# Prompt index products of a hybrid decoder layer: full rows, and index queries held for one tile

## The chip, the cores and the metric

The kernel runs on one core of one Trainium2 chip. It is written by hand for the five engines, each with its own instruction stream: PE (TensorE), DVE (VectorE), ACT (ScalarE), POOL (GpSimd) and SP (SyncE, which here only issues transfers). Semaphores order them. The metric is the device time of one execution in microseconds; three timed runs of the kernel before gave 3959.62, 3966.36 and 3967.23 us, a median of 3966.36.

## The reference

One decoder layer over 2048 prompt tokens and 64 sample tokens: a combined projection, then attention over keys that an indexer picks, beside a state-space branch, an output projection and a squared-relu MLP. The change touches the indexer for the prompt:

```python
def indexer_topk(qi, wi, ki, q_pos, topk):
    s = jnp.einsum('bqhd,bld->bqhl', qi, ki) * (IDX_DIM ** -0.5)      # 4 heads of 64
    score = jnp.einsum('bqhl,bqh->bql', jax.nn.relu(s), wi) * (N_IDX_HEADS ** -0.5)
    score = jnp.where(admissible[None], score, -jnp.inf)
    _, idx = lax.top_k(score, topk)                                    # topk = 256
```

For every block of 128 queries this is done against all keys up to the block's end. All of it is in float32. The four heads share one set of index keys of 64 dimensions. Positive factors on the score change nothing in the choice, and the kernel leaves them out.

## The kernel before

The prompt is cut into 16 tiles of 128 tokens. Tiles 0 and 1 need no choice. The others are chosen in four groups, `SELECT = ((2, 3), (4, 5, 6, 7), (8, ..., 11), (12, ..., 15))`. A tile passes through three steps of a search pipeline: its scores are made, then ACT counts the upper 19 bits of a threshold while the next tile's scores are made, then DVE counts the lower 13 bits and builds the mask while a third tile's scores are made. The third of these steps is shared by no more than three tiles, so `score` has three buffers.

Scores of a tile `t` are made in pieces, `(h, u)`: head `h` of 4, and a stretch `u` of 1024 keys, that is up to two banks of 512. A piece is one `matmul` per bank on PE (`index`, line 1567), one relu per bank on ACT (line 1889, from PSUM into `relu`, two buffers), and one multiply-and-add with the head's weight on DVE (`combine`, line 2159). PSUM banks of the products are a ring of four, `sring`, made of the banks `sc` and `tr` that attention uses at other times. A 32-bit product is recorded as two LDWEIGHTS and two MATMUL records, whose buffer names are `kiT` (keys) and `qi` (queries).

`kiT` holds the 64 dimensions of the index keys twice, in partitions 0 to 63 and 64 to 127. The queries are in DRAM as `qi_d[t]`, 128 partitions x 2 x 128: partitions 0 to 63 hold heads 0 and 2, partitions 64 to 127 heads 1 and 3. A product for head `h` takes the half `h % 2` of both, 64 rows:

```python
rows = slice(HD * (h % 2), HD * (h % 2) + HD)
pe.matmul(sring[i % SRING][:, 0:w], qi[rows, n % 2, h // 2, :], R["kiT"][rows, 512 * b:512 * b + w], ...)
```

The order of all work is one list, `plan`, that every engine walks through in the same order, each doing its own part of a unit. It merges the main stream, the units of the projection and the MLP (`W`, `N`, `M`, `U` for an up chunk of 24 products, `D` for down products, `E`), with the side stream, units of search `("S", s, p, k)` and of attention `("A", s, j)`, by rough costs. In `("S", s, p, k)`, `s` is the group, `p` the step of the pipeline and `k` the tick within it. While `p` is 0, a piece goes out at every tick; from `p` = 1 on, at every second tick of 20, since search rounds lie between. The last piece of a group's first tile and the first piece of its second are thus next to each other in the plan: for tiles 4 and 5 nothing lies between, nor for tiles 2 and 3 and tiles 8 and 9; for tiles 12 and 13 one `D` unit of twelve down products does. Tile 8's pieces have one up unit in their midst, and tile 9's first piece has one right behind it.

SP walks the same plan and issues transfers in order; where it has to wait, all that is behind it waits too. `load_index` (line 1345) is one of them, beside weights (`raw`, line 1279), features (`xs`), masks and queries of attention. At the start of a group it first waits until attention's last outputs of the group before are stored (line 1385), since both use the same memory. `qi` has two buffers with a semaphore each, so tile t+1's queries are asked for while tile t's predecessor is in work.

Of the kernel before, what the change touches and what calls it, by code (L numbers as in the profile page):

```python
# [6 lines left out]
ACT = mybir.ActivationFunctionType  # L7
# [7 lines left out]
P = 128  # L15
# [11 lines left out]
HD = 64  # L27
# [393 lines left out]
class Count:  # L421
# [9 lines left out]
    def wait(self):  # L431
        self.eng.wait_ge(self.sem, self.n)
# [350 lines left out]
def blend(nc, A, ident, par):  # L783
# [262 lines left out]
    with ExitStack() as ctx:  # L1046
# [32 lines left out]
        at[0] = side  # L1079
        qi = place_at("qi", [P, 2, 2, P])  # L1080
        relu = place_at("relu", [P, 2, 1024])
# [119 lines left out]
        x2_st, y_st = [sem(f"x2_st{i}_") for i in range(5)], [sem(f"y_st{i}_") for i in range(5)]  # L1201
        qi_ld, mask_st = [sem("qi_ld0_"), sem("qi_ld1_")], [sem("mask_st0_"), sem("mask_st1_")]
        s_full, s_free, comb_ok, causal_ok, trial_ok, count_ok, mask_ok, own = (
# [63 lines left out]
        with nc.Block() as block:  # L1267
            @block.sync
            def _(sp):
# [75 lines left out]
                def load_index(t):  # L1345
                    n = turn_s[t]
                    if n >= 2:
                        sp.wait_ge(s_full, n_index[t])
                    sp.dma_start(qi[:, n % 2], A["qi_d"][t]).then_inc(qi_ld[n % 2], 16)

                n_index, seen = {}, []
                for ts in SELECT:
                    for t in ts:
                        seen.append(t)
                        n_index[t] = index_bank[seen[-3], NIH - 1, banks(seen[-3]) - 1] + 1 if len(seen) > 2 else 0

# [23 lines left out]
                def select_part(s, p, k):  # L1380
                    ts = SELECT[s]
                    if p == 0 and k == 0:
                        if s:
                            for i in range(2):
                                sp.wait_ge(aT_st[i], 16 * 2 * s)
                        load_index(ts[0])
                        load_index(ts[1])
                    if 1 <= p and k == 0 and p + 1 < len(ts):
                        load_index(ts[p + 1])
                    if p >= 2 and k == LOWER + CHOICE - 1:  # L1390
                        t = ts[p - 2]
                        n = turn_s[t]
                        sp.wait_ge(mask_ok, n + 1)
                        sp.dma_start(m_d[t, :, 0:width(t)], tie[:, 0:width(t)]).then_inc(mask_st[n % 2], 16)
# [93 lines left out]
            def _(pe):  # L1488
# [78 lines left out]
                def index(s, p, k):  # L1567
                    ts = SELECT[s]
                    if p >= len(ts) or k % piece_step(p) or k // piece_step(p) >= len(pieces(ts[p])):
                        return  # L1570
                    t = ts[p]
                    h, u = pieces(t)[k // piece_step(p)]
                    n = turn_s[t]
                    pe.wait_ge(qi_ld[n % 2], 16 * (n // 2 + 1))
                    rows = slice(HD * (h % 2), HD * (h % 2) + HD)
                    for b in range(2 * u, min(2 * u + 2, banks(t))):
                        i = index_bank[t, h, b]
                        wait(pe, s_free, i - SRING + 1)
                        w = part_w(width(t), 512, b)
                        pe.matmul(sring[i % SRING][:, 0:w], qi[rows, n % 2, h // 2, :], R["kiT"][rows, 512 * b:512 * b + w],  # L1580
                                  start=True, stop=True).then_inc(s_full, 1)
# [180 lines left out]
            def _(act):  # L1762
# [114 lines left out]
                def select_part(s, p, k):  # L1877
# [3 lines left out]
                    if p < len(ts) and k % piece_step(p) == 0 and k // piece_step(p) < len(pieces(ts[p])):  # L1881
# [4 lines left out]
                        for b in range(2 * u, min(2 * u + 2, banks(t))):  # L1886
                            i, w = index_bank[t, h, b], part_w(width(t), 512, b)
                            act.wait_ge(s_full, i + 1)
                            act.activation(relu[:, r % 2, 512 * (b - 2 * u):512 * (b - 2 * u) + w], sring[i % SRING][:, 0:w],
                                           ACT.Relu).then_inc(s_free, 1)  # L1890

# [590 lines left out]
```

## Time and profile before

| | |
|---|---|
| median of three runs | 3966.36 us |
| profiled execution | 3963.13 us, its span 3961.5 us |
| PE busy | 3229.5 us, 82% |
| DVE / ACT / POOL busy | 2167.9 / 1850.8 / 1266.4 us |
| mean granted clock of PE | 0.891 of full |
| index products, in the two groups of records of 512 columns | 224 records, 131.8 us |
| loads of `qi` | 14, of 128 KB each |

The span is the time between the first and the last record; the execution's own time is a little longer. Busy shares are means over a kernel that has stages of different kinds: the input projection up to about 350 us, the state-space branch up to about 560, the sample tokens and the first search up to about 1040, then three rounds in which search and attention lie beside the MLP, and from about 3050 us on the last quarter of the MLP. Index products lie between 569 and 2782 us. The granted clock in the slices is a mean over 99 us each: 9 or less means that some of the slice was spent at the lower level.

### The profile page before, as it was taken

How to read it: one execution, taken by the hardware profiler on the slowest of the kernel's cores; microseconds unless marked ns; L12 is line 12 of the kernel's file. 1: busy time of each engine (PE TensorE's matmuls, PEld its weight loads, DVE VectorE, ACT ScalarE, POOL GpSimd, SP SyncE). 2: the span in 40 equal slices, each digit the busy share in tenths (PEclk: the TensorE clock that was granted, in tenths of full speed). 3: DMA queues.
4: the chain of work that ended last, by engine and by line, in shares of the span. 5: the costliest groups of instructions: out<-in, count | busy, mean ns of one | idle time of the engine just before them, and what ended most of it. 6: DMA issues, size and time to landing. Idle time of an engine off the chain costs nothing.

```text
span 3961.5 us, 47273 instructions
## 1 busy us (share of the span) xinstructions
PE 3229.5 (82%) x15388; PEld 2447.5 (62%) x15388; DVE 2167.9 (55%) x4196; ACT 1850.8 (47%) x3065; POOL 1266.4 (32%) x1134
## 2 busy tenths in 40 slices
PE   7996536258778899886888998777788999889997
PEld 6885422134555677654666776555566777668885
DVE  4434934942357864367886333677785333553334
ACT  3323325513456645565664446656654444433333
POOL 1334401122024541243254013422463110324544
PEclk9997768577889889988899999988898999989998
DMA  4444245344232221123222111242222110432222
GB/s 155 138 138 160 50 144 136 86 153 148 83 124 66 69 83 51 48 70 141 73 81 73 52 33 57 69 148 69 69 69 85 38 42 25 147 117 80 80 85 72
DMA packets 198864, 357.36 MB, mean 90 GB/s; under 512 B 55690, under 2 KB 113100, under 8 KB 197180
## 3 DMA queue, kind: packets, MB, share of 16 engines
q1 hardware_dynamic: 180092, 327.81, 25.9%
q0 software_dynamic: 9312, 18.14, 1.4%
q10 hardware_dynamic: 9216, 8.39, 0.7%
q8 instruction: 124, 2.03, 0.2%
q14 instruction: 120, 0.98, 0.1%
HBM read 294.44 MB, written 67.01 MB: 91 GB/s over the span
## 4 chain that ended last, share of the span: by engine, by line
PE 42%; DVE 20%; issue 11%; ACT 6%; POOL 3%; DMA 2%; SPq 1%; ACTq 1%; POOLq 0%; DVEq 0%
PE r L1564 9%; PE r L1532 8%; PE po L1613 7%; PE r L1505 3%; PE tr L1604 3%; DVE junk_v_b L2233 3%; PE sc L1592 3%; DVE trial_b L2185 3%; POOL acc_b L1999 2%; DVE dn_b L2080 2%; DVE up_b L2080 2%; PE sc L1591 2%; ACT junk_a_b L1874 1%; ACT dn_b L1769 1%; PE r L1676 1%
## 5 line engine op out<-in xcount | busy, mean ns | idle before, releaser
L1564 PE MATMUL r<-dn_b,h_b 128*128 128x512 f32 x2880 | 767.6, 424 | 174.9 <-ACT part_b L1825 84.7
L1564 PEld LDWEIGHTS r<-dn_b,h_b 128*128 128x128 f32 x2880 | 574.9, 205 | 353.9 <-ACT part_b L1825 103.3
L1999 POOL TENSOR_TENSOR acc_b<-acc_b,part_b 128x512 f32<-128x512 f32 x375 | 514.5, 1392 | 605.4 <-ACT part_b L1825 604.8
L1532 PE MATMUL r<-x_hi_b,up_b 128*128 128x512 f32 x2048 | 660.8, 396 | 6.8 <-DVE x_lo_b L2099 4.2
L1874 ACT ACTIVATE junk_a_b<-score_b,trial_b 128x384 int8<-128x384 f32 (+13 forms) x266 | 348.1, 1309 | 303.5 <-DVE trial_b L2185 291.8
L1532 PEld LDWEIGHTS r<-x_hi_b,up_b 128*128 128x128 f32 x2048 | 389.6, 190 | 105.5 <-issue 15.6
L1980 POOL TENSOR_TENSOR hr_b<-hr_b 128x512 f32<-128x512 f32 x128 | 146.6, 1145 | 852.9 <-ACT hr_b L1812 852.9
L1532 PE MATMUL r<-x_lo_b,up_b 128*128 128x512 f32 x1024 | 402.8, 393 | 0.0
L1825 ACT ACTIVATE part_b<-r 128x512 f32<-128x512 f32 x390 | 224.4, 594 | 239.6 <-PE r L1564 163.2
L1903 ACT ACTIVATE pT_b<-tr 128x512 f32<-128x512 f32 (+3 forms) x320 | 169.0, 528 | 331.9 <-PE tr L1604 330.2
L1613 PE MATMUL po<-V_sb,pT_b 128*128 128x64 f32 x2176 | 314.0, 285 | 1.7 <-DVE o_b L2250 1.4
L1613 PEld LDWEIGHTS po<-V_sb,pT_b 128*128 128x128 f32 x2176 | 272.1, 194 | 66.7 <-issue 53.8
L2080 DVE TENSOR_TENSOR dn_b<-raw_b,dn_b 128x1024 fp32r<-128x1024 f32 x120 | 171.9, 1433 | 237.3 <-ACT dn_b L1769 236.3
L2080 DVE TENSOR_TENSOR up_b<-raw_b,up_b 128x1024 fp32r<-128x1024 f32 x136 | 196.7, 1446 | 190.6 <-ACT up_b L1769 190.0
L2264 DVE CUSTOM_DVE_ANT_0 prob_b<-sc,mk_b,mx_b 128x512 f32<-128x512 f32 (+3 forms) x192 | 125.0, 651 | 306.2 <-PE sc L1592 306.1
L2233 DVE TENSOR_SCALAR_CACHE_REDUCE junk_v_b<-score_b,trial_b 128x384 bf16<-128x384 f32 (+13 forms) x182 | 268.0, 1472 | 1.3
L1988 POOL TENSOR_TENSOR h_b<-hr_b,h_b 128x512 fp32r<-128x512 f32 x128 | 219.6, 1716 | 132.1 <-ACT h_b L1841 132.1
L1532 PEld LDWEIGHTS r<-x_lo_b,up_b 128*128 128x128 f32 x1024 | 195.1, 190 | 39.1
L2264 DVE CUSTOM_DVE_ANT_0 prob_b<-sc,mk_b 128x512 f32<-128x512 f32 (+3 forms) x128 | 82.2, 642 | 242.4 <-PE sc L1592 218.4
L1909 ACT ACTIVATE prob_b<-prob_b,nmx_b 128x128 f32<-128x128 f32 (+15 forms) x128 | 153.9, 1202 | 110.4 <-DVE nmx_b L2270 108.8
L1604 PE MATMUL tr<-ident_sb,prob_b 128*128 128x128 f32 x1088 | 181.0, 283 | 12.5 <-ACT prob_b L1909 11.7
L375 PE MATMUL pp<-w_hi_sb,xT_hi_sb 128*128 128x512 f32 (+2 forms) x512 | 178.9, 349 | 5.9 <-ACT w_raw_sb L203 5.9
(385 smaller groups left out, 5749.7 us busy)
## 6 DMA issues: line engine op xcount, KB each, us to landing
raw_b<-w_up SPq DMA_DIRECT2D x128, 512.0 KB, 3.7
raw_b<-w_down SPq DMA_DIRECT2D x128, 512.0 KB, 3.6
raw_b<-w_out SPq DMA_DIRECT2D x64, 256.0 KB, 3.0
kv_b<-kv_pages SPq DMA_DIRECT2D x96, 128.0 KB, 3.8
kv_b<-kv_pages POOLq DMA_DIRECT2D x96, 128.0 KB, 3.7
x_tok_sb<-x_all SPq DMA_DIRECT2D x17, 512.0 KB, 4.6
xT_sb<-xT_all SPq DMA_DIRECT2D x17, 512.0 KB, 4.9
kic<-kidx_d SPq DMA_DIRECT2D x4, 2048.0 KB, 8.8
```

The source lines that it names most:

```text
L375: mm = pe.matmul(pp[j][:, 0:b - a], x[:, t % 2, k, :], w[:, k, a:b], start=n == 0, stop=n == 3 * KD - 1)
L1532: mm = pe.matmul(x[:], wt[:, c], y[:, k], start=k == n == 0, stop=(k, n) == (KD - 1, 2))
L1564: mm = pe.matmul(x[:], f[:, tok], w[:, col], start=c == n == 0, stop=(c, n) == (KQ - 1, 2))
L1604: mm = pe.transpose(x[:, (k - 4 * b) * P:(k - 4 * b + 1) * P], prob[:, n % 2, k * P:(k + 1) * P], ident[:])
L1613: mm = pe.matmul(po[:, h, :], pT[:, prob_no[t, h, b] % 3, k - 4 * b, :], R["V"][:, k, n:n + HD], start=k == 0, stop=k == t)
L1825: act.activation(dst, ring[bank_no[key] % RING][:], ACT.Copy).then_inc(free_act, 1)
L1874: act.activation(junk_a[:, 0:width(t)], score[:, n % 3, 0:width(t)], ACT.Sign, bias=trial[:, 0:1].bitcast(F32), accum_out=count[:, 0:1]).t ...
L1988: pool.tensor_tensor(z, s, a.bitcast(F32), ALU.subtract).then_inc(h_lo_ok, 1)
L1999: pool.tensor_tensor(dst, dst, part[:, add_no[key] % 2, :], ALU.add).then_inc(add_pool, 1)
L2080: dve.tensor_tensor(lo, raw_of(x), hi.bitcast(F32), ALU.subtract).then_inc(lo_ok, 1)
L2233: c.step(dve.tensor_scalar(junk_v[:, 0:width(t)], score[:, turn_s[t] % 3, 0:width(t)], trial[:, lower_trial(t)].bitcast(F32), 0.0, ALU.is_ ...
L2264: dve.tensor_tensor_reduce(out=prob[:, n % 2, 512 * b:512 * b + w], in0=sc[i % 2][:, 0:w], in1=mk[:, t % 2, 512 * b:512 * b + w], scale=1. ...
```

## The change

Three things are changed. First, each head's queries are placed in both halves of the partitions, so `qi` is `[P, NIH, P]` and holds one tile instead of two, in the same room. A product then takes all 128 rows: the keys stand twice in `kiT`, so the sum is twice the product, and the relu behind it has `scale=0.5`. Second, `load_index` issues four transfers of 64 partitions x 2 x 128 in place of one of 128 x 256: two halves of the partitions, for the even and the odd heads each. Third, as there is one buffer, a tile's load waits until the last product of the tile before it has ended, and it stands in the plan behind the last piece of that tile instead of one tile earlier; there is one semaphore, `qi_ld`, that counts 64 per tile.

```diff
-        qi = place_at("qi", [P, 2, 2, P])
+        qi = place_at("qi", [P, NIH, P])
...
-        qi_ld, mask_st = [sem("qi_ld0_"), sem("qi_ld1_")], [sem("mask_st0_"), sem("mask_st1_")]
+        qi_ld, mask_st = sem("qi_ld"), [sem("mask_st0_"), sem("mask_st1_")]
...
                 def load_index(t):
-                    n = turn_s[t]
-                    if n >= 2:
-                        sp.wait_ge(s_full, n_index[t])
-                    sp.dma_start(qi[:, n % 2], A["qi_d"][t]).then_inc(qi_ld[n % 2], 16)
+                    wait(sp, s_full, n_index[t])
+                    for z in range(2):
+                        for h in range(2):
+                            sp.dma_start(qi[HD * z:HD * z + HD, h::2], A["qi_d"][t, HD * h:HD * h + HD]).then_inc(qi_ld, 16)
...
-                        n_index[t] = index_bank[seen[-3], NIH - 1, banks(seen[-3]) - 1] + 1 if len(seen) > 2 else 0
+                        n_index[t] = index_bank[seen[-2], NIH - 1, banks(seen[-2]) - 1] + 1 if len(seen) > 1 else 0
...
                         load_index(ts[0])
-                        load_index(ts[1])
-                    if 1 <= p and k == 0 and p + 1 < len(ts):
+                    if p + 1 < len(ts) and k == len(pieces(ts[p])) * piece_step(p):
                         load_index(ts[p + 1])
...
-                    pe.wait_ge(qi_ld[n % 2], 16 * (n // 2 + 1))
-                    rows = slice(HD * (h % 2), HD * (h % 2) + HD)
+                    pe.wait_ge(qi_ld, 64 * (n + 1))
...
-                        pe.matmul(sring[i % SRING][:, 0:w], qi[rows, n % 2, h // 2, :], R["kiT"][rows, 512 * b:512 * b + w],
+                        pe.matmul(sring[i % SRING][:, 0:w], qi[:, h, :], R["kiT"][:, 512 * b:512 * b + w],
                                   start=True, stop=True).then_inc(s_full, 1)
...
-                                           ACT.Relu).then_inc(s_free, 1)
+                                           ACT.Relu, scale=0.5).then_inc(s_free, 1)
```

On SP's queue at the start of the third group (tiles 8 and 9), with what each transfer waits for, the order before is this. `raw_b` are weights, `a_d` is attention's last output.

```order
L1378 DMA a_d<-aT_b 128x512 [waits tr_free_b]
L1349 DMA qi_b<-qi_d 128x256 [waits s_full_b,aT_st1__b,aT_st0__b]
L1349 DMA qi_b<-qi_d 128x256 [waits s_full_b]
L1279 DMA raw_b<-w_down 128x1024 [waits lo_ok_b]
L1349 DMA qi_b<-qi_d 128x256 [waits s_full_b]
L1279 DMA raw_b<-w_down 128x1024 [waits lo_ok_b]
```

The two loads in a row are those of tiles 8 and 9, the third is tile 10's. Now the same stretch of SP's queue reads:

```order
L1378 DMA a_d<-aT_b 128x512 [waits tr_free_b]
L1349 DMA qi_b<-qi_d 64x2x128 [waits s_full_b,aT_st1__b,aT_st0__b]
L1349 DMA qi_b<-qi_d 64x2x128 x3
L1279 DMA raw_b<-w_down 128x1024 [waits lo_ok_b]
L1349 DMA qi_b<-qi_d 64x2x128 [waits s_full_b]
L1349 DMA qi_b<-qi_d 64x2x128 x3
L1279 DMA raw_b<-w_down 128x1024 [waits lo_ok_b]
```

The second block of four is now tile 9's and has moved behind one load of weights; its wait on `s_full` is for tile 8's last product. Tile 10's has moved further down, out of this stretch.

PE's order does not change, only the semaphore in front of the products. At tiles 4 and 5 (tile 4's last two heads, tile 5's first, and the output projection behind them) PE had this:

```order
L1580 MATMUL sc<-kiT_sb,qi_b 128x128 [waits s_free_b]
L1580 MATMUL tr<-kiT_sb,qi_b 128x512 [waits s_free_b,qi_ld0__b]
L1580 MATMUL tr<-kiT_sb,qi_b 128x128 [waits s_free_b]
L1580 MATMUL sc<-kiT_sb,qi_b 128x512 [waits s_free_b,qi_ld1__b]
L1580 MATMUL sc<-kiT_sb,qi_b 128x256 [waits s_free_b]
L1505 MATMUL r<-x_hi_b,dn_b 128x512 [waits f_lo_b]
```

And it has this after the change:

```order
L1578 MATMUL sc<-kiT_sb,qi_b 128x128 [waits s_free_b]
L1578 MATMUL tr<-kiT_sb,qi_b 128x512 [waits s_free_b,qi_ld_b]
L1578 MATMUL tr<-kiT_sb,qi_b 128x128 [waits s_free_b]
L1578 MATMUL sc<-kiT_sb,qi_b 128x512 [waits s_free_b,qi_ld_b]
L1578 MATMUL sc<-kiT_sb,qi_b 128x256 [waits s_free_b]
L1504 MATMUL r<-x_hi_b,dn_b 128x512 [waits f_lo_b]
```

The product of tile 5 (the one before the row of 256 columns) waited for a buffer of its own, `qi_ld1`; it now waits for a count that only transfers issued after tile 4's last product can bring.

## Rows read from the trace of the kernel before

**Rows 1.** The page's head, busy time by engine, and slices of busy share and clock.
```profile
span 3961.5 us, 47273 instructions
...
PE 3229.5 (82%) x15388; PEld 2447.5 (62%) x15388; DVE 2167.9 (55%) x4196; ACT 1850.8 (47%) x3065; POOL 1266.4 (32%) x1134
...
PEclk9997768577889889988899999988898999989998
```

**Rows 2.** Index products (line 1580): durations in ns, and idle time before them.
```profile
L1580 PE MATMUL sc<-kiT_sb,qi_b x152: 269/589/1219, 569.1 to 2764.3; 64*128 64x512 f32 x124, 64*128 64x384 f32 x12, 64*128 64x128 f32 x8, 64*128 64x256 f32 x8
...
  DMA qi_b<-qi_d: 53.9, 7
```

**Rows 3.** Chain that ended last, tiles 2 and 3: start us, us, what.
```profile
560.84 8.13 DMA qi_b<-qi_d
...
575.70 0.48 ACT relu_b L1889
```

**Rows 4.** The same chain at tiles 4 and 5.
```profile
1060.14 3.28 DMA qi_b<-qi_d
...
1072.14 7.15 PE r L1505 x24
```

**Rows 5.** The same chain at tiles 8 and 9.
```profile
1611.52 2.06 DMA qi_b<-qi_d
1613.62 1.99 PE sc L1580 x3
...
1618.26 5.67 PE r L1532 x24
...
1632.51 0.97 ACT relu_b L1889 x2
```

**Rows 6.** The same chain at tile 12.
```profile
2393.47 2.10 DMA qi_b<-qi_d
```

**Rows 7.** PE and ACT in time behind tile 12: start us, us, instruction, idle before.
```profile
2408.11 3.04 PE L1564 MATMUL r<-dn_b,h_b 128*128 128x512 f32 x12
...
2413.80 1.68 ACT L1874 ACTIVATE junk_a_b<-score_b,trial_b 128x1664 int8<-128x1664 f32 x1 [2.70 <-POOL score_b L2028]
```

**Rows 8.** Loads of the index queries on SP: issue in ns, landing in us.
```profile
L1349 SPq DMA_DIRECT2D qi_b<-qi_d x14: 319/430/433, 560.8 to 2514.7; - x14
...
DMA to landing us min/median/max: 2.0/3.2/8.1
```

**Rows 9.** The chain again, index and down products of the third group.
```profile
1649.68 2.00 PE tr L1580 x2
...
1653.39 8.30 PE r L1564 x24
...
1691.51 8.05 PE r L1564 x24
...
1721.60 1.91 PE sc L1580 x4
1723.51 5.66 PE r L1564 x24
```

**Rows 10.** PE in time, gate products of the state-space branch (all 128 rows).
```profile
648.82 16.43 PE L1719 MATMUL r<-zb_b,wglu_b 128*128 128x512 f32 x34 [28.29 <-DMA zb_b<-z_d]
```

**Rows 11.** PE in time, the first records of tile 4.
```profile
1063.46 1.22 PE L1580 MATMUL sc<-kiT_sb,qi_b 64*128 64x512 f32 x1 [4.64 <-DMA qi_b<-qi_d]
1063.57 1.19 PE L1580 MATMUL tr<-kiT_sb,qi_b 64*128 64x512 f32 x1
```

**Rows 12.** Busy us of each engine in stretches; third number from the end is PE's clock.
```profile
1061.60:1075.30 13.70, 11.52 (x28) 7.17 (x29) 4.15 (x7) 6.05 (x15) 0.29 (x1) 0.50 0.11 34
1614.60:1618.00 3.40, 3.40 (x9) 1.54 (x7) 0.87 (x2) 1.44 (x4) 0.00 (x0) 0.50 0.03 5
...
1648.70:1659.00 10.30, 10.30 (x20) 5.89 (x19) 3.54 (x5) 4.77 (x10) 5.87 (x5) 0.50 0.00 0
...
1686.30:1696.50 10.20, 10.20 (x20) 5.83 (x19) 3.54 (x5) 4.88 (x9) 5.55 (x5) 0.50 0.00 1
...
2590.80:2604.40 13.60, 12.02 (x23) 7.34 (x24) 9.24 (x22) 8.29 (x15) 4.70 (x3) 0.50 0.54 193
```

## The prediction

> **What bounds the kernel now.** The views were read in this order: the page's head and slices, the chain that ended last, the group of the index products, the queue that loads their queries, and then stretches by granted clock. The span is 3961.5 us and the profiled execution took 3963.13 us; the median of the three timed runs is 3966.36, 3.2 above it. PE is busy for 82% of the span, at a clock that keeps moving between its two levels, 2.4 GHz (1.00 in the rows) and 1.2 GHz (0.50) [rows 1]. No engine is the bound throughout: in the search phases the chain goes from PE to ACT to DVE to POOL and back.
>
> The index products read 64 of 128 rows. They are 304 records, two to a 32-bit product, and PE stood idle 53.9 us in all in front of seven of them for the load of `qi` [rows 2]. At the four places where a new group of tiles begins (tiles 2, 4, 8, 12) the chain itself goes through that load and the burst of products behind it [rows 3 to 6]. Hence anything added to either lies on the path that sets the end. Within a search phase, in contrast, the next tile's queries are asked for many products ahead.
>
> **Part 1: one load becomes four.** The loads of `qi` took 0.43 us each to issue and 2.0 us at least, 3.2 in the median, to land [rows 8]. The first product of a group now waits for the fourth issue instead of the first: 3 x 0.4 = +1.2 us, four times. At tile 2 the load took 8.1 us to land, behind others on the queue [rows 3], so that part of this is hidden there; I take 0.8.
>
> **Part 2: one buffer instead of two.** Tile t+1's queries are asked for only when the last product of tile t has ended. In the middle of a search the load stands at step 16 of 20 (step 8 for tiles up to 7), with several up or down units before the first use: over 10 us, against 1.2 + 3.2 us for four issues and a landing, so zero. SP's following weight loads wait for the low part of a split that DVE makes after the combine of that same last product, so no load is held up for it; bound 0 to 1 us. But behind the first tile of a group only the rest of one step lies between. There PE waits 0.1 (hand-over) + 1.2 (issues) + 2.1 (landing [rows 5]) = 3.4 us, and ACT's relu, in order, waits behind it. Between ends of 2.0 and 8.1 us for a landing I take the one nearest in place.
>
> **Part 3: full rows instead of halves.** The price of one product does not depend on its rows: a bank of 512 columns is 0.95 us at full clock (four 64-row records, two banks, 1.91 us [rows 9]) and 34 full-row records of the same type and width took 16.43 us, 0.48 each, again 0.97 a bank [rows 10]. At the low level it is 2.0 us [rows 9]. What goes is that two heads with different row halves ran beside each other: the first records of heads 0 and 1 start 0.11 us apart and both take 1.2 us [rows 11]. This only matters where heads follow each other at once, in the first tile of each group.
>
> That rule is in the Trainium skill, page "TensorE: Matmul & The Clock Gate", Part 3 on packing small matmuls: products on different row groups run concurrently. By it alone two halves would double the pace, and the bursts of tiles 2, 4, 8 and 12 (30 banks, 28.5 us at full clock) would lose 14 us instead of the 6 or so of the sum below; the trace agrees that they overlap, but only partly, since ACT and the ring of four banks pace the rest. The sum uses the places' own rows.
>
> **Part 4: the clock.** Index products with half the rows do not lift the clock as fast as others. From 1061.6 to 1075.3 PE was busy 11.5 of 13.7 us, most of it with index products one head after another, and the clock stayed at 0.50; from 1648.7 to 1659.0 and from 1686.3 to 1696.5 PE was busy all the time at 0.50, and it rose only after down products had run. In the burst from 1613.62, where both halves of the rows were in use, the clock was back by 1618.0, 4.4 us after the start [rows 5, 12]. If it is rows in use that count, full rows bring it back earlier. On the chain two places gain: 24 down products took 8.30 and 8.05 us, and 5.66 at full clock, and the second bank before them 0.8 us each: 2.6 + 2.4 + 1.6 = 6.6 us [rows 9]. Elsewhere the low stretches lie around idle PE, which rows do not change.
>
> **The sum, by place.** Burst: 4.4 us at low clock (2.2 banks), the rest at 0.95 a bank.
> - Tiles 2, 3: four products of 384 columns are 3 banks, 4.4 + 0.8 = 5.2 us from 569.9, ending at 575.1; + 3.4 + 0.95 gives tile 3's first bank at 579.4, and ACT took it at 575.70 [rows 3]: +3.7.
> - Tiles 4, 5: 5 banks, 4.4 + 2.7 = 7.1 from 1064.7, ending at 1071.8; + 3.4, and 1.5 banks between the levels 2.2: 1077.4. The 24 output-projection products began at 1072.14 [rows 4]. They keep their 7.15 us, since the new gap lets the clock fall again: +5.2.
> - Tiles 8, 9: 9 banks, with an up unit of 5.67 us between. Product start +1.2; the first 4.25 banks take 6.35 us, to 1621.2 instead of 1618.26; the up unit to 1626.8; 4.75 banks to 1631.3; + 3.4 + 1.9 for tile 9's first piece: 1636.6, relu done at 1637.1, where it was 1633.5 [rows 5]: +3.6.
> - Tiles 12, 13: 13 banks from 2396.8: 4.4 + 10.3, to 2411.5 instead of 2408.1, where the burst had begun 2.1 us after the load at 2393.47 [rows 6, 7]. Twelve down products (3.0 us) cover most of the gap, and ACT comes to tile 13 only after its count at 2413.8 [rows 7]: +3.4.
>
> Delay 15.9 us. Two things make it smaller: records of a dense burst follow at less than the 0.95 of a piece that starts from rest (the 34 records carry start-up at low clock), say 1 us over 30 banks; and tile 4's products gain a clock that rises at 1069 instead of 1075.3 for what follows, say 2. So +13, and -6.6 for part 4: +6.4. The scale inside relu costs nothing: the same ACTIVATE with another immediate.
>
> 3963.1 + 6.4 = 3969.5 for such an execution, 3972.8 against the median. Bounds: 0 (every gap hidden, nothing gained) and, with landings of 3.2 to 8.1 us, another 5 to 10.
>
> **Rivals.**
> 1. The clock does not care for rows: full bursts and gaps are paid and nothing comes back, and new gaps of 3.4 us let the clock fall after tiles 4 and 8 (1.7 us each). 13 + 1.7 = +14.7: 3981. For it: long low stretches begin at idle PE, and the gaps add idle. Against it: ten busy microseconds at 0.50 twice [rows 12]. The Trainium skill, same page, Part 1, says that activity releases the throttle and counts PE as busy or not, without rows. By that rule this rival would hold; the trace speaks against it, as said.
> 2. Faster: the clock gains in more than two stretches, and the bursts hardly grow. The low stretch from 2590.8 to 2604.4 has 12.0 us of busy PE [rows 12]; if full rows end it after its first products, some 7 us of it run at the higher level and give 3.5. The one from 1061.6 on may give another 3 beyond the 2 counted, and two more of that kind in the last two search phases 1.7 each: 10 in all. If ACT (0.5 us for a bank's relu [rows 3]) and DVE's combine paced the bursts of nine and thirteen banks anyway, 3 of the 13 go. 13 - 3 - 6.6 - 10 = -6.6: 3960. It decides where the gain from the clock passes 10 us. Against: the chain in 2590 to 2604 lies mostly on ACT and POOL, and low stretches mostly begin at an idle PE.
> 3. The change does nothing that can be seen: loads are hidden behind the count of the earlier tile, which ACT does first, and both effects are small: 3966.
>
> **How the numbers follow.** A difference under 0.2% (7.9 us) can't be told from none. Chances: forecast (3973; its own range 3967 to 3980, from 2 us either way on each of the two larger gaps and 3 on the clock) 0.42; rival 1 0.21; rival 2 0.19; rival 3 0.18. Slower by over 0.2% (above 3974.3) are 0.18 of the forecast's 0.42 and nearly all of rival 1, 0.38 together. Faster (below 3958.4) are two thirds of rival 2 and a little of rival 3: 0.14. The same: 0.48. A tenth is left out at each end: 3957 to 3985.
>
> **What would show it.** Idle PE in front of index products "until DMA qi" rising from 53.9 us in 7 to about 68 in some 8 to 10; SP's queue waiting on index products; the relu of tiles 3, 5 and 9 first later by 3 to 5 us relative to the load of tiles 2, 4 and 8; the pairs of records 0.1 us apart gone; full clock within some 4 us of an index product where it took ten; the 24 down products behind tile 9's product at 1653 near 5.7 us. Wrong would be: a landing above 5 us, a gap in mid-search, or the same 0.50 over full-row products.

## The result, and the profile after

The changed kernel took 3982.17 us (median of 17 runs, 3973.7 to 3995.83), the kernel before 3968.16 us in 17 runs of its own: a ratio of 1.0034, 95% interval 1.0024 to 1.0045, so 14.0 us slower. The profiled execution took 3977.22 us, 14.1 more than the one before.

The head of the page after, which answers to [rows 1] (span; busy us, share and instructions of each engine; PE's clock in 40 slices):

```profile
span 3975.5 us, 47315 instructions
...
PE 3224.3 (81%) x15388; PEld 2462.2 (62%) x15388; DVE 2161.6 (54%) x4196; ACT 1853.2 (47%) x3065; POOL 1264.4 (32%) x1134
...
PEclk9998768577888889988889999988888999989998
```

PE is busy for 5.2 us less in a span that is 14.0 us longer: the added time is idle time. The view of the index products, which answers to [rows 2], and the loads on SP, which answer to [rows 8]:

```profile
L1578 PE MATMUL sc<-kiT_sb,qi_b x152: 271/592/1222, 569.3 to 2778.2; 128*128 128x512 f32 x124, 128*128 128x384 f32 x12, 128*128 128x128 f32 x8, 128*128 128x256 f32 x8
...
  DMA qi_b<-qi_d: 99.0, 15
```
```profile
L1349 SPq DMA_DIRECT2D qi_b<-qi_d x56: 512/602/654, 560.7 to 2637.1; - x56
...
  PE sc L1578: 63.2, 8
  PEld sc L1578: 35.7, 7
...
DMA to landing us min/median/max: 2.1/2.2/7.2
```

A record lasts as long with 128 rows as with 64 (median 592 ns against 589); that the records stand closer together with 128 rows is shown behind e10. The idle time in front of the products has nearly doubled, from 53.9 to 99.0 us; PE's matmuls have 63.2 of it at eight places (41.4 at four before), the queue of weight loads beside them the rest of the same waits. The eight are each group's first tile, as before, and each group's second tile, which is new. Each issue takes 0.60 us where the one of twice the size took 0.43. The chain after at tiles 2 and 3, which answers to [rows 3]:

```profile
560.72 0.57 SPq L1349
...
562.68 6.52 DMA qi_b<-qi_d
...
569.34 2.90 PE sc L1578 x4
...
572.86 2.58 PE tr L1578 x4
...
575.45 0.51 SPq L1349
...
577.30 2.22 DMA qi_b<-qi_d
...
579.56 3.78 PE sc L1578 x4
```

The first tile's products end at 575.43 and the second tile's begin at 579.56: 4.1 us, of which 1.85 are the first three issues and 2.22 the fourth with its landing. The products then run at the lower level, 3.78 us for two banks. At tiles 8 and 9 the chain, which answers to [rows 5], has both again:

```profile
1620.02 0.54 SPq L1349
...
1621.89 2.22 DMA qi_b<-qi_d
...
1624.15 3.78 PE sc L1578 x4
...
1630.82 5.46 PE r L1531 x24
...
1640.41 0.52 SPq L1349
...
1642.26 2.20 DMA qi_b<-qi_d
...
1644.50 3.80 PE sc L1578 x4
```

Tiles 12 and 13, which answer to [rows 6, 7], have more than that:

```profile
2419.00 0.87 PE tr L1578 x2
...
2421.21 0.95 ACT up_b L1767
...
2422.19 1.24 DVE up_b L2078
...
2423.44 0.33 SPq L1279
...
2423.82 0.52 SPq L1349
...
2425.67 2.56 DMA qi_b<-qi_d
...
2428.28 3.74 PE sc L1578 x4
```

Tile 12's last product ended at 2419.87, but SP stood at a load of raw weights (L1279) that waits for DVE's split, and came to tile 13's queries only at 2423.82. What the change seems to give back is seen in PE's timeline behind tile 9, where before 24 down products took 8.30 us in the chain [rows 9]:

```profile
1667.51 6.16 PE L1563 MATMUL r<-dn_b,h_b 128*128 128x512 f32 x24
```

To compare all runs, six stretches were read from every trace, each between the same two events. **A**, tiles 2 and 3: from the issue of the sample queries ahead of tile 2's load to ACT's `rl_b` behind tile 3. **B**, tiles 4 and 5: from an issue of `xs_b` to a split on DVE behind them. **C**, tile 8 to tile 9's first piece: from ACT's `part_b` (1609.35 before) to POOL's `hr_b` (1634.05). **D**, what follows, up to a count of ACT (1706.32). **E**, tiles 12 and 13: from an issue of `raw_b` (2388.43) to ACT's `part_b` (2416.91). **F**, from there to POOL's `h_b` (2440.04). "Lead" is the number of transfers for a group's first tile.

| trace (rows of the products; buffers; lead) | A | B | C | D | E | F |
|---|---|---|---|---|---|---|
| before (64; 2; 1) | 27.0 | 40.4 | 24.7 | 72.3 | 28.5 | 23.1 |
| before, again | 27.2 | 40.7 | 26.3 | 65.5 | 28.5 | 23.1 |
| e10 (64; 2; 1) | 26.7 | 40.2 | 26.2 | 65.3 | 27.1 | 23.3 |
| e6 (64; 2; 4) | 27.7 | 41.9 | 29.8 | 65.6 | 31.8 | 23.3 |
| e6, again | 27.7 | 41.6 | 27.8 | 70.3 | 31.5 | 23.3 |
| e1 (64; 1; 4) | 30.4 | 46.0 | 31.9 | 70.3 | 35.1 | 23.1 |
| after (128; 1; 4) | 33.2 | 43.6 | 31.7 | 65.1 | 36.3 | 21.6 |
| e4 (128; 1; 4, earlier) | 33.1 | 45.0 | 31.6 | 65.1 | 32.0 | 21.6 |
| e3 (128; 1; 2) | 31.7 | 42.6 | 27.3 | 66.3 | 35.0 | 21.6 |
| e9 (128; 1; 2, earlier) | 31.8 | 42.0 | 30.5 | 66.0 | 30.0 | 21.6 |
| e2 (128; 2; 4) | 29.2 | 39.0 | 28.5 | 65.0 | 31.1 | 21.6 |
| e5 (64 first, then 128; 2; 4) | 27.4 | 39.3 | 27.8 | 65.2 | 30.9 | 21.6 |
| e7 (64 first, then 128; 2; 1) | 27.0 | 38.5 | 24.7 | 65.6 | 28.4 | 23.1 |
| e7, again | 27.3 | 38.3 | 24.8 | 65.4 | 28.2 | 21.6 |

After against before these are +6.2, +3.2, +7.0, -7.1, +7.9 and -1.5: +15.6 (with the second decimals), of 14.0 more span. The rest of the program gives 1.6 back in sum. Outside these stretches, traces of kernels that are alike there differ by more than 20 us in arrival: `part_b` of stretch C comes at 1609.35 in one trace of the kernel before and 23.7 us later in the other. So single traces are compared by stretches, and whole runs by their ratios.

### The profile page after: what moved, and what is told of

It is laid out like the page before. It is cut to its first block, busy times and chain, and to the rows that moved or that the text cites. A ratio compares the mean times of both kernels' runs of the same rounds, so it can differ in the third digit from the quotient of the medians.

```text
span 3975.5 us, 47315 instructions
## 1 busy us (share of the span) xinstructions
PE 3224.3 (81%) x15388; PEld 2462.2 (62%) x15388; DVE 2161.6 (54%) x4196; ACT 1853.2 (47%) x3065; POOL 1264.4 (32%) x1134
## 4 chain that ended last, share of the span: by engine, by line
PE 43%; DVE 19%; issue 11%; ACT 5%; POOL 4%; DMA 2%; SPq 1%; ACTq 1%; POOLq 0%; DVEq 0%
PE r L1563 10%; PE r L1531 9%; PE po L1611 7%; PE tr L1602 3%; DVE junk_v_b L2231 3%; PE sc L1590 3%; PE r L1504 3%; DVE trial_b L2183 3%; POOL acc_b L1997 2%; DVE dn_b L2078 2%; DVE up_b L2078 2%; PE sc L1589 2%; PE sc L1578 1%; ACT junk_a_b L1872 1%; PE r L1674 1%
## 5 line engine op out<-in xcount | busy, mean ns | idle before, releaser
L2231 DVE TENSOR_SCALAR_CACHE_REDUCE junk_v_b<-score_b,trial_b 128x384 bf16<-128x384 f32 (+13 forms) x182 | 267.9, 1472 | 1.3
```

Source lines behind the costliest of these rows:

```text
L2231: c.step(dve.tensor_scalar(junk_v[:, 0:width(t)], score[:, turn_s[t] % 3, 0:width(t)], trial[:, lower_trial(t)].bitcast(F32), 0.0, ALU.is_ ...
```

## The experiments

**The theory and its rivals.** The theory: the change loses by waits for loads (four issues ahead of each group's first tile, and a second tile whose queries can't be asked for earlier), and gains by rows, since the clock comes back sooner when products use 128 of them. The rivals: the clock doesn't care for rows (the prediction's first rival), and the full-row bursts of the first tiles are the loss, not the waits. A third rival was not thought of beforehand: that 128 rows save time on PE directly, without the clock; it is taken up behind e10. Each ratio below is to the kernel before in the same series of runs; its median was 3964.94 us (29 runs) beside e1 to e4, 3965.43 (29) beside e5 to e9, and 3965.02 (35) beside the last four.

**e1, half rows.** Loads and buffer of the change, products of 64 rows.

```diff
-pe.matmul(..., qi[:, h, :], R["kiT"][:, 512 * b:512 * b + w], ...)
+rows = slice(HD * (h % 2), HD * (h % 2) + HD)
+pe.matmul(..., qi[rows, h, :], R["kiT"][rows, 512 * b:512 * b + w], ...)
-               ACT.Relu, scale=0.5)
+               ACT.Relu)
```

> The changed kernel with 64-row products again: each head reads its own half of the rows (head h the half h % 2), relu without its scale; the loads (one buffer, four transfers, asked for behind the last product of the tile before) stay as changed. My theory: the change lost time by its loads and got part of it back by the clock (traces: 7.1 us between 1650 and 1700, where the low stretches of 10.2 us shrank to 3.4), so without the full rows this is as slow as the change or slower: 15 to 20 us over before (ratio 1.004 to 1.005); clock low for about 10 us again behind tile 9's first products. Rival A (the clock does not care for rows, and side-by-side heads are what was lost): 6 to 9 us over before, clearly faster than the change, and no longer low stretch than with full rows.

Measured: 3989.79 us, ratio 1.0053 (1.0036 to 1.0069), against the change's 1.0034. PE's idle time in front of the products is the change's (98.3 us). The direction is that of the theory: the rows bring a gain, and the loads are a larger loss than the whole. The two intervals overlap, though, and these are six runs of another series, so this pair alone would not show it. Stretches B and F are 2.4 and 1.5 us longer than after; A is 2.8 shorter. The 24 down products behind tile 9, in PE's timeline:

```profile
1684.48 7.07 PE L1563 MATMUL r<-dn_b,h_b 128*128 128x512 f32 x24
```

**e2, two buffers.** Full rows and four transfers, but a second buffer (in an idle part of `score` and 1 KB more for each partition), and loads in the order of before.

```diff
-pe.wait_ge(qi_ld, 64 * (n + 1))
+pe.wait_ge(qi_ld[n % 2], 64 * (n // 2 + 1))
...
-                        load_index(ts[0])
-                    if p + 1 < len(ts) and k == len(pieces(ts[p])) * piece_step(p):
+                        load_index(ts[0])
+                        load_index(ts[1])
+                    if 1 <= p and k == 0 and p + 1 < len(ts):
```

> The changed kernel with full rows and four transfers per tile, but with two buffers and each load asked for as early as before the change (the second buffer lies in unused columns of a score buffer and in 1 KB of room of its own). My theory: the waits of PE at tiles 3, 5, 9 and 13 (3 to 4 us each) go, and the later first load of each group (1.8 to 2.6 us, three transfers of 0.60 us) and the longer bursts stay, against the clock's gain: -3 to +4 us against before (ratio 0.999 to 1.001). Rival A (what was lost is the overlap of heads in the bursts, not the waits): still 8 to 12 us over before.

Measured: 3966.39 us, ratio 0.9997 (0.9979 to 1.0014), and the idle time is 62.6 us in 7 waits. A, B, C and E are 4.1, 4.7, 3.1 and 5.3 us shorter than after, 17.1 in sum: the later loads of the second tiles are what the change loses.

**e3, two transfers.** The change with one transfer for each half of the partitions.

```diff
-                        for h in range(2):
-                            sp.dma_start(qi[HD * z:HD * z + HD, h::2], A["qi_d"][t, HD * h:HD * h + HD]).then_inc(qi_ld, 16)
+                        sp.dma_start(qi[HD * z:HD * z + HD].rearrange("p (a h) q -> p a h q", h=2),
+                                     A["qi_d"][t].rearrange("(h p) a q -> p a h q", h=2)).then_inc(qi_ld, 16)
...
-pe.wait_ge(qi_ld, 64 * (n + 1))
+pe.wait_ge(qi_ld, 32 * (n + 1))
```

> The changed kernel with two transfers per tile instead of four (one for each half of the partitions, 64 x 2 x 2 x 128). My theory: issue time counts at eight places (the first load of each group and the one behind its first tile), so two issues of 0.60 us less at each give 1.2 x 7 to 8 = 8 to 9 us back: 5 us over before (ratio 1.001 to 1.002). Rival B (the time of an issue goes by its pieces, not by transfers, so that two cost as much as four, 1.2 us each): no difference to the change, 13 us over before.

Measured: 3966.61 us, ratio 0.9996 (0.998 to 1.0012). The loads on SP:

```profile
L1348 SPq DMA_DIRECT2D qi_b<-qi_d x28: 573/620/647, 560.7 to 2628.0; - x28
...
DMA to landing us min/median/max: 2.5/3.0/7.4
```

An issue costs about the same for twice the bytes (0.62 against 0.60 us), while the landing took 0.4 us more at least. At stretch C the chain shows what else came of it:

```profile
1636.82 0.58 SPq L1348
...
1637.44 2.67 DMA qi_b<-qi_d
...
1640.15 2.00 PE sc L1578 x4
```

The wait is 3.4 instead of 4.1 us, and the products behind it took 2.00 us for two banks instead of 3.78: in this execution the clock had not fallen. The stretches give 7 us less than after (1.6, 1.0, 4.3, 1.4, less 1.1 at D), the ratios 0.0038 or 15 us. In this trace a place for the other half lies outside the six stretches, in attention between 1450 and 1472 us before. The same 82 matmul records took this long after (first row) and in e3 (second row; stretch, its length, busy us by engine, PE's clock):

```profile
1458.63:1480.56 21.93, 21.93 (x82) 17.29 (x82) 6.99 (x17) 8.17 (x16) 2.80 (x2) 0.61 0.23 67
...
1464.44:1478.77 14.33, 14.33 (x82) 11.43 (x82) 5.99 (x17) 7.94 (x17) 3.04 (x2) 1.00 0.25 90
```

The clock did not fall there in e3, which is worth 7.6 us; in all thirteen other traces the stretch took 21.9 to 23.3 us. The mean granted clock of e3's twelve runs (0.892, against 0.889 in the change's 17) suggests that its profiled execution was no exception. Why fewer issues lead to this, some 370 us behind tile 5's wait, is open.

**e4, load ahead.** The change, with the load of each group's second tile one tick earlier, ahead of the raw weights.

```diff
-if p + 1 < len(ts) and k == len(pieces(ts[p])) * piece_step(p):
+if p + 1 < len(ts) and k == (len(pieces(ts[p])) * piece_step(p) if p else len(pieces(ts[p])) - 1):
```

> The changed kernel with the load for a group's second tile one tick earlier in the plan, right behind the first tile's last piece, so that at tile 13 it stands ahead of the load of weights that waits for DVE. It still waits for the last product of the first tile. My theory: at tile 13 the load was issued 3.9 us after the last product of tile 12 because SP stood at that load of weights; this returns, PE waits 1 to 2 us there instead of 6, and 2.5 to 4 us of the kernel go: 10 us over before (ratio 1.0025). The other three places don't change. Rival C (tile 13's load is not on the path, ACT's count is): no difference to the change.

Measured: 3976.7 us, ratio 1.0029 (1.0015 to 1.0043), E at 32.0 instead of 36.3 us. Behind tile 12's last product (ending at 2419.88) no issue stands in the chain any more, only ACT's relu and what was late before:

```profile
2419.01 0.87 PE tr L1578 x2
...
2420.46 0.27 ACT relu_b L1887
...
2423.34 1.89 DVE score_b L2167
...
2428.98 7.21 PE r L1563 x30
```

So the order on SP cost 4.3 us at this one place. The ratio (0.0005 below the change's) can neither confirm nor deny a gain of that size.

**e5, half rows first.** As e2, with 64 rows in each group's first tile.

```diff
+rows = slice(HD * (h % 2), HD * (h % 2) + HD) if p == 0 else slice(0, P)
-ACT.Relu, scale=0.5)
+ACT.Relu, scale=0.5 if p else 1.0)
```

> The change with two buffers of index queries, as the second experiment, and with products of 64 rows (relu without the factor) in the first tile of each group, of 128 rows in all others. The loads stay four transfers per tile. My theory (the first tile's products lose by 128 rows, as two heads can't lie side by side, and the clock's gain at tiles 8 and 9 needs full rows only from tile 9 on): the stretch of tile 8 is 1 to 2.5 us shorter than with full rows throughout (28.5), the stretch behind tile 9 stays at 65 us (72.3 before), the whole run 3 to 5 us below the second experiment's, ratio to the kernel before about 0.999. Rival (the clock needs full rows in tile 8 as well): the stretch behind tile 9 goes back to 70 to 72 us and the run is 0 to 4 us slower than the second experiment's. Rival (rows don't matter in the first tile): all stretches as in the second experiment, ratio 0.9997.

Measured: 3958.79 us, ratio 0.9985 (0.9973 to 0.9997); A is 1.8 and C 0.7 us shorter than in e2, D the same. The direction is as expected and the stretch less than expected. A short D does not need full rows in tile 8.

**e6, half rows, two buffers, and once more.** As e2 with 64 rows throughout: of the change only the four transfers are left.

```diff
+rows = slice(HD * (h % 2), HD * (h % 2) + HD)
+pe.matmul(..., qi_of(n, h)[rows, :], R["kiT"][rows, 512 * b:512 * b + w], ...)
```

> Products of 64 rows everywhere as before, relu without the factor, two buffers; of the change only the four transfers per tile are left. My theory (the issue of four transfers stands ahead of the first product of a group, four times, at 2.0 us in place of 0.43): 1.4 to 2 us longer at each of the four places that begin a group, none elsewhere, the stretch behind tile 9 at 70 to 72 us, the run 5 to 8 us slower than before, ratio 1.0013 to 1.002. Rival (the issue is hidden behind other waits and full rows are what lengthened the first tiles): ratio 1.000, tile 8's stretch at 24.7 us. Rival (two buffers in themselves, not full rows, brought the stretch behind tile 9 down): that stretch at 65 us here too, ratio below 0.9995.

> The sixth kernel once more (64 rows everywhere, two buffers, four transfers), for a second profile. Its first one had 65.6 us behind tile 9, with 64 rows, against what I expected of rows. If the rows decide and that profile was a chance, 70 us or more here. If the later start of tile 8 decides (its first load takes longer), 65 to 66 again. If the two buffers do, 65 to 66 as well, but then the kernel before, which has two too, must show it as well. Ratio 1.0005 again, within 0.001.

Measured: 3967.43 us, ratio 1.0005 (0.9996 to 1.0014), and the second time 3969.76 us, ratio 1.0009 (0.9995 to 1.0024). A and B are 0.5 to 0.7 and 0.9 to 1.5 us longer than before. E is 3.0 to 3.3 us longer, and C 28.8 us in the mean of two traces against 25.5, 3.3 longer. e6 and e5 were run in one series and differ only by the rows behind each group's first tile: 8.6 us between their medians. What I had not expected is D: 65.6 us with 64 rows in the first trace, and 70.3 in the second one of the same kernel. The down products behind tile 9 in the second:

```profile
1663.47 6.95 PE L1569 MATMUL r<-dn_b,h_b 128*128 128x512 f32 x24
...
1700.81 7.05 PE L1569 MATMUL r<-dn_b,h_b 128*128 128x512 f32 x24
```

**The kernel before, once more.** No edit.

> The kernel before, unchanged, once more, for a second profile of it: is the long stretch behind tile 9's products (72.3 us in the first profile, 20 us of it at the lower clock) the same each time? If the rows of the products decide it, 70 to 72.3 us again, and a ratio of 1.000 within 0.001. If it hangs on where the clock's fall happens to come in the one execution, another value between 65 and 72, as likely 65 as 72.

Measured: 3967.01 us, ratio 1.0005 (0.9992 to 1.0017), D at 65.5 us. The groups that took 8.30 and 8.05 us [rows 9]:

```profile
1677.93 5.74 PE L1564 MATMUL r<-dn_b,h_b 128*128 128x512 f32 x24
...
1712.33 5.74 PE L1564 MATMUL r<-dn_b,h_b 128*128 128x512 f32 x24
```

The long stretch of the first profile is thus one of several outcomes that a kernel with 64 rows has: 72.3, 65.5, 65.3, 65.6, 70.3 and 70.3 us in six traces, 68.2 in the mean. The eight traces with 128 rows behind the first tile have 65.0 to 66.3, 65.5 in the mean, and none is long. A rule that all 64-row kernels lose there is refuted. Three long ones of six against none of eight speak against a clock whose course doesn't depend on rows, but do not exclude it at this one place; what is left of the gain is 2.7 us in the mean, not 7.

**e7, the first tile as before, and once more.** Two buffers; a group's first tile by one transfer and with 64 rows, all others in both halves and with 128.

```diff
+                    if n in FIRST:
+                        sp.dma_start(qi[:, 0:2], A["qi_d"][t]).then_inc(qi_ld[0], 16)
+                    for z in range(0 if n in FIRST else 2):
...
+rows = slice(0, P) if p else slice(HD * (h % 2), HD * (h % 2) + HD)
+lhs = qi_of(n, h) if p else qi[rows, h // 2, :]
...
+                                           ACT.Relu, scale=0.5 if p else 1.0).then_inc(s_free, 1)
```

> Two buffers; a group's first tile is loaded and multiplied as before the change (one transfer of 128 x 256, 64 rows), all other tiles in both halves by four transfers and with 128 rows. My theory (all losses of the change are the waits for loads and the first tile's four transfers, its only gain is the clock behind tile 9): the stretches of tiles 2 and 3, 8 and 12 at the values before (27.0, 24.7, 28.5 us, within 1), the stretch behind tile 9 at 65 us in place of 72.3, the run 5 to 9 us faster than the kernel before, ratio about 0.998. Rival (what is gained at tiles 8 and 9 is given back later by the clock, since the sum over a stage stays the same): ratio 0.9995 to 1.0005 with the same short stretch. Rival (the clock needs full rows in tile 8 too): that stretch at 70 to 72 us, ratio 1.000.

> The seventh kernel once more (two buffers, the first tile as before the change, 128 rows in the others), for a second profile and a narrower ratio: 0.9968 in six runs. If the gain is real, 0.9965 to 0.9985 again and 65 to 66 us behind tile 9. If it was the luck of few runs, 0.999 or above.

Measured: 3953.89 us, ratio 0.9968 (0.9956 to 0.998), and the second time 3955.01 us, ratio 0.998 (0.9966 to 0.9993). This beats both kernels, by 8 to 13 us against before by the ratios. A, C and E are those of before, B is 2 us shorter, D never long. In the second trace:

```profile
1622.78 2.04 DMA qi_b<-qi_d
...
1629.48 5.68 PE r L1541 x24
```
```profile
1663.66 6.17 PE L1573 MATMUL r<-dn_b,h_b 128*128 128x512 f32 x24
```

**e10, e7 with half rows.** All loads and buffers of e7, 64 rows in all products.

```diff
+rows = slice(HD * (h % 2), HD * (h % 2) + HD)
+lhs = qi_of(n, h)[rows, :] if p else qi[rows, h // 2, :]
```

> The seventh kernel with 64 rows in all products (relu without the factor) and all its loads and buffers. Theory of the rows (128 rows in the tiles behind the first bring the clock back sooner): slower than the seventh by 5 to 11 us, ratio to before 1.000, within 0.001, 70 to 72 us behind tile 9. Rival (the layout of loads and buffers, or where the clock's fall happens to come, made the seventh kernel fast): as the seventh, ratio 0.997 to 0.9985, 65 to 66 us behind tile 9.

Measured: 3964.91 us, ratio 1.0002 (0.9988 to 1.0016), beside e7's 0.998 in the same series: 9.9 us between the medians, that only the rows of the products in the later tiles can make. The intervals of the two ratios overlap slightly. e6 and e5, whose intervals do so too, make the same comparison with four transfers for the first tile and have 8.6 us; two pairs that agree leave little room for chance. The ratio was expected; the 70 to 72 us at D were not (65.3, a short outcome). The places that show a gain are B (1.8 us less in e7), D (2.7 in the mean) and F (23.1 to 23.3 us in all six traces with 64 rows, 21.6 in seven of eight with 128). That is some 6 us. A seventh stretch, **G**, has most of the rest: from the end of B to a count of ACT that starts at 1349.91 before (tiles 5 to 7). In the table's order it took 249.8, 256.3, 249.8, 256.4, 256.1 and 256.2 us in the six traces with 64 rows, and 247.4 to 250.2 in the eight with 128: 4.7 us less in the mean. Here too 64 rows have a short and a long outcome and 128 rows do not.

**How the rows do it: two effects, of which the theory has one.** The clock's course is different: the part of G from 1250.44 to 1270.82 took 20.4 us at full clock in two traces with 64 rows and 25.5 at a mean of 0.75 in four, and 22.1 to 22.4 at 0.85 or 0.86 in all eight with 128. F is at a mean of 0.93 before and at 1.00 after. But the records also stand closer together when all rows are used. In the chain, at two pieces of tile 6 between down products, both at full clock, before:

```profile
1183.70 1.70 PE tr L1580 x4
1185.40 2.95 PE r L1564 x12
1188.35 1.70 PE sc L1580 x4
```

And after:

```profile
1191.97 1.50 PE tr L1578 x4
1193.47 2.75 PE r L1563 x12
1196.22 1.50 PE sc L1578 x4
```

A piece and twelve down products go from 4.65 to 4.25 us. From the record ahead of a piece to the fourth behind it, 32 of the pieces behind the first tiles take 0.39 us less (0.38 to 0.40) in all eight traces with 128 rows than in all six with 64, whether the piece has one bank or two. Where the clock is low it is more: at 1252.76 before, the same distance is 5.71 us in four of the 64-row traces and 4.3 to 4.6 in the 128-row ones. With 64 rows the weight load of the down product behind such a piece starts 0.41 us after the piece's last matmul; with 128 rows both start together (1184.92 and 1185.33 before, 1192.98 and 1192.99 after).

An estimate from these rows: 32 x 0.39 = 12.5 us of PE's time, of which the run keeps only what lies on its path. The mean granted clock of e10's twelve runs is 0.890 and of e7's eleven in the same series 0.890, so the faster kernel has no larger share of full clock. How the 9.9 us are divided between the two effects, and whether the clock's course follows the rows themselves or the changed spacing, no run here separates.

**e9, two transfers and ahead.** The change with the edits of e3 and e4 together.

```diff
...
-pe.wait_ge(qi_ld, 64 * (n + 1))
+pe.wait_ge(qi_ld, 32 * (n + 1))
...
-if p + 1 < len(ts) and k == len(pieces(ts[p])) * piece_step(p):
+if p + 1 < len(ts) and k == (len(pieces(ts[p])) * piece_step(p) if p else len(pieces(ts[p])) - 1):
```

> The change with one buffer as it is, but two transfers per tile in place of four, and the load of a group's second tile one place earlier in the order, ahead of the raw weights. My theory (what holds SP ahead of the second tile's load costs 3.5 us at tile 13 alone, and the issue of four transfers costs 1 us or more at each of seven to eight waits; the two add up): 3 to 5 us below the experiment with two transfers, so 15 to 20 us below the change, ratio to before about 0.999. Rival (the two overlap, since a load that is issued earlier also finds its queue free): as the experiment with two transfers, ratio 0.9996 or above.

Measured: 3967.62 us, ratio 1.0002 (0.999 to 1.0014), where 0.999 was expected: no gain over e3 in the whole run. At E it is there (30.0 against 35.0 us), at C 3.2 us are lost. Nor has e9's trace the attention at full clock that e3's has (22.0 us instead of 14.3). The gain of the earlier place in the order is shown at its stretch; that it shortens a run is not.

## Why the prediction was right, and where its terms were off

The sign and the kind of cost were right: 3982.17 us lies in the range (3957 to 3985), slower than forecast by 9 us, near its upper end. The forecast's own range (3967 to 3980) missed it by 2 us; that the wider one holds it is owed to the room given to the rivals. Of the prediction's +6.4 for an execution, +14.1 were measured. The delays (loads, waits and longer bursts) were put at 13 us and came to 25.9 (6.2 + 4.8 + 7.0 + 7.9 at A, B, C and E, with B taken without its gain); the gains were put at 6.6 us and came to 10.2 in this pair of traces (7.1 at D, 1.5 at F, 1.6 at B). With the means over all traces they are 1.6 + 2.7 + 1.5 + 4.7 (G) = 10.5, and 25.9 - 10.5 = 15.4 beside the 14.0 of the runs. So the delays were twice what was put down, and gains at places that the sum did not name (most of B, F and G) made up for part of it: that part is luck.

- **Part 1, one load becomes four.** Sized at 3 x 0.4 = 1.2 us. Three issues are 0.54 + 0.60 + 0.60 and their hand-overs, 1.87 us, and the last lands 0.15 later: from the first issue to the first product 4.1 us at tile 8 where it was 2.1. The duration was taken from an issue of 128 x 256, and a smaller transfer of another shape costs more, not less. At tile 2 the slow landing hid most of it, as said (8.62 us against 8.26). e6 shows more than the load's own 2 us at C and E (3.3 in the mean and 3.0 to 3.3); why is open.
- **Part 2, one buffer.** The mechanism and the places were right: four new waits, none in mid-search. Sized at 3.4 us, they are 4.1 to 4.2, by the same issues. Not foreseen: the products behind a wait run at the lower clock, 3.8 us for two banks where 1.9 was put in for a piece. At tile 3 and tile 9 this is 1 and 1.9 us.
- **Part 2 at tile 13** is the step of the loads that failed: "no load is held up for it", with a bound of 0 to 1 us, asked what stands behind the load and not what stands ahead of it. The new place of tile 13's load is behind a load of raw weights that waits for DVE's split, and DVE for ACT. SP came to it 3.9 us after the last product of tile 12, so the twelve down products could not cover the gap. Sized at 3.4 for the place, it was 7.9; e4 takes 4.3 of it away.
- **Part 3, full rows in the bursts.** The bursts came out nearly right: tile 8's part up to the up unit 6.7 us (6.35 forecast), tile 12's whole burst 13.9 (14.7), tile 2's 6.1 (5.2, all at the lower clock). Against each one's kernel before, e5 is 0.0012 or 4.8 us below e2, with intervals that overlap; the stretches give 2.4. Its premise, "the price of one product does not depend on its rows", is wrong. The 34 full-row records that gave 0.97 us a bank ran in part at the low clock; in tile 12's burst after the change 3.25 banks took 2.80 us, 0.86 a bank. And a 64-row piece between other products holds PE 0.39 us longer than one of 128 rows (see behind e10), in the tiles for which the prediction gave the rows no price of their own.
- **Part 4, the clock.** It was right that rows count in the run, and that the 24 down products behind tile 9 would come near 5.7 us (6.16). The size, 6.6 us, was read off one profiled execution, as was the whole of it in the first trace (7.1); in the mean over traces it is 2.7 us. What it missed was elsewhere: "they keep their 7.15 us" is wrong at tiles 4 and 5 (1083.46 in the chain after: 5.59 us for the 24 products), and stretch F gains 1.5. The ten busy microseconds at 0.50 that it leaned on are real, but not constant: the mean clock over D was 0.83 in the first trace and 0.95 in b2. The Trainium skill, page "TensorE: Matmul & The Clock Gate", Part 1, counts activity as PE busy or not. The 9.9 us between e10 and e7 do not refute that, since rows also change how closely PE's records follow each other.
- **Tiles 4 and 5** came out as forecast for the delay (the 24 products began 5.4 us later against tile 4's load, +5.2 forecast), and 1.6 better by the clock, as the 24 products took 5.59 instead of 7.15 us.
- **What would show it**: idle time 99.0 us instead of 68, since the view counts a wait twice, for matmuls and for weight loads (8 places, as said); 63.2 us for the matmuls alone, where it was 41.4. Relative to the load of the group's first tile, the first relu of tile 3 came 6.2 us later instead of 3 to 5, that of tile 5 4.3, that of tile 9 5.8.

```profile
581.73 0.60 ACT L1887 ACTIVATE relu_b<-sc 128x512 f32<-128x512 f32 x1 [3.87 <-PE sc L1578]
```

Rival 1 had the time nearly right (3981) for a wrong reason: its bursts and gaps were paid, but the rows did give something back. Rival 2's extra gains exist, 7.8 us of the 10 it asked for (B, F and, in the mean, G), but not where it looked: the products of the stretch that was at 2590.8 to 2604.4 still ran at the low clock in the trace after (4.5 us from the record ahead of the piece to the fourth behind it, where it is 2.6 at full clock).

## What to carry to other kernels

When a load moves in the order of a queue, look at what stands ahead of it as well as behind: what it is queued after, what that waits for, and in which state the clock is when its consumer starts at last. A change that needs room should keep its old form where its cost is exposed (here the first tile of a group) and take the new one where the work is hidden. Here that needed a second buffer, 1 KB more for each partition, which with the loads in their old order took the change's 0.34% back (e2); the old form in the first tiles then brought the gain of 0.2 to 0.3%. A gain that is read from the clock's low stretches in one profile needs a second profile of the same kernel before it goes into a sum. And the price of an operand's shape is read from when the next instruction starts, not from how long the record lasts.

## What the runs showed of the hardware

- With products of 64 rows the clock's course behind the same instructions differs between executions of one kernel: 8.37 or 5.74 us for the same 24 down products (the kernel before, two traces). With 128 rows ahead of them the group took 6.15 to 6.34 us in the traces read, neither so short nor so long. The mean granted clock over the runs was the same, 0.890, for e7 and e10.
- SP's issue of 64 partitions x 2 x 128 took 0.60 us, of 128 x 256 0.43 us, and of the doubled form of e3 0.62 us: the shape counts here, not the bytes.
- A 32-bit record of 512 columns lasts the same with 64 and 128 rows, 589 and 592 ns in the median. But a piece of two to four 64-row records between records of 128 rows held PE 0.39 us longer at full clock than the same piece with 128 rows, in 32 places of all 14 traces.
